# Expert rows scattered to their token's place and read back plainly, empty slots skipped, alpha in the first norm's parameters

## The chip, the cores and the metric

The kernel runs on one core of one Trainium2 chip. The metric is device microseconds of one execution, the median of the runs. The engines are TensorE (PE, with its weight loads PEld), VectorE (DVE), ScalarE (ACT), GpSimd (POOL) and SyncE (SP, which here only issues transfers). A transfer issued by SyncE or ScalarE goes through a queue of its own (q1, q10), one issued by GpSimd through q0; 16 transfer engines serve all queues.

## The reference

The reference is one inference step of a decoder trunk of two layers for 512 prompt tokens and 64 sample tokens, together T = 576 tokens of D = 1024 numbers, all in float32. Cut to what matters here:

```python
def hier_moe(x, w_group, b_group, w_expert, b_expert, w_gate_up, w_down):
    ...
    top_vals, top_idx = lax.top_k(e_in_group, TOP_K_INNER)
    top_w = jax.nn.softmax(top_vals, axis=-1) * g_w[:, None]
    expert_id = g_idx[:, None] * EXPERTS_PER_GROUP + top_idx
    combine = jnp.sum(jax.nn.one_hot(expert_id, N_EXPERTS, dtype=jnp.float32) * top_w[..., None], axis=1)
    hgu = jnp.einsum("td,edf->tef", xt, w_gate_up)
    gate, up = jnp.split(hgu, 2, axis=-1)
    a = jax.nn.silu(gate) * up * combine.astype(x.dtype)[:, :, None]
    y = jnp.einsum("tef,efd->td", a, w_down)
    ...
        x = layer_norm(DEEPNORM_ALPHA * x + mix, ln1_g[i], ln1_b[i])
        moe = hier_moe(x, moe_w_group[i], moe_b_group[i], moe_w_expert[i], moe_b_expert[i],
                       moe_w_gate_up[i], moe_w_down[i])
        x = layer_norm(DEEPNORM_ALPHA * x + moe, ln2_g[i], ln2_b[i])
        gate = jax.nn.sigmoid(jnp.einsum("bsd,de->bse", x, ple_w_gate[i]) + ple_b_gate[i])
        x = x + gate * jnp.einsum("bsp,pd->bsd", p[i], ple_w_proj[i])
```

There are 16 experts, each token uses two, so a layer has 2 x 576 = 1152 pairs of token and expert. An expert has a gate_up matrix of 1024 x 512 and a down matrix of 256 x 1024.

## The kernel before

Every product is made of three products of high and low halves. ScalarE writes the high half of a weight unit (`w_hi`, line 678), VectorE the low half (`w_lo`, line 944). A unit is 128 x 2048 numbers, 1 MiB, in one of four buffers `w_raw`; SyncE loads unit d once unit d - 4 is split. An expert has three units, two for gate_up and one for down.

A layer runs its mixer, then the first norm (token tiles of 128, the fifth of 64), the router, the experts, the second norm and the gated projection (PLE). The code is written out for each engine, and semaphores order the engines; no scheduler moves anything.

First norm and router: TensorE turns the rows, ScalarE normalises them into `x_tok`, and GpSimd multiplies and adds the norm's parameters `ln_params` (lines 604 and 609, tile 3 on VectorE), then stores the rows in memory, `x_scratch` (line 598). The parameters are loaded at line 594. VectorE computes the ranks of tokens in their experts; a matrix product turns them into `slot_token`: for each expert 128 slots that hold the number of a token. An empty slot holds 0, so it gathers token 0's row. Line 1196 copies this table from PSUM.

Experts: GpSimd gathers the 128 rows of a slot tile from `x_scratch` into one of two buffers `x_gathered` (line 619, all 16 gathers in a row, each from the third on waiting until TensorE turned the tile before the last). TensorE's step s (`moe_step`, line 1736) is gate_up of expert s, turning the slots of s + 1 (line 1689), down of expert s - 1, turning the activations of s. ScalarE and VectorE write the halves `xgT_hi` and `xgT_lo` (lines 797 and 1245), the activation with SiLU (line 819), and ScalarE copies the result out of PSUM to `expert_y` (line 804) and issues its store to `y_scratch` (line 806), at row 128 s. `expert_y` has one buffer: the next copy waits for the store. Before the first expert ScalarE multiplies all of `x_tok` by alpha, lines 830 and 831. Where an expert has over 128 tokens, an overflow part runs under an `If`; with the reference's inputs it doesn't run.

Second norm: GpSimd waits for all stores and gathers for each of five token tiles twice the 128 rows that belong to its tokens (line 646, places in `token_slot`) into `y_gathered`, which has room for four tiles. VectorE adds both to `x_tok` with their weights (line 1309) and takes statistics; for tiles 3 and 4 ScalarE weights the first rows (line 872) and GpSimd adds them (line 653). ScalarE normalises, TensorE turns the rows. SyncE has issued the loads of `ple_w_gate` before and goes on to `b_w_in` of the next mixer in layer 0.

## Time and profile before

| | |
|---|---|
| median of 3 runs | 1434.43 us (1432.51 to 1435.21) |
| the profiled execution | 1434.39 us, span 1432.9 us |
| TensorE busy | 1278.4 us, 89% of the span |
| VectorE busy | 808.0 us, 56% |
| ScalarE busy | 582.6 us, 41% |
| GpSimd busy | 207.5 us, 14% |
| mean transfer rate | 170 GB/s, 244.25 MB |

The page gives shares of the whole span. The stages differ: the experts of the first layer run from about 598 to 776 us, those of the second from about 1144 to 1320 us. In the slices of part 2 these stand out by their GB/s. A timeline row gives the start of an operation or a run of equal ones, the time it took, the line, what it writes and reads, and in brackets how long its engine had been idle and what ended that.

### The profile page before, as it was taken

How to read it: one execution, taken by the hardware profiler on the slowest of the kernel's cores; microseconds unless marked ns; L12 is line 12 of the kernel's file. 1: busy time of each engine (PE TensorE's matmuls, PEld its weight loads, DVE VectorE, ACT ScalarE, POOL GpSimd, SP SyncE). 2: the span in 40 equal slices, each digit the busy share in tenths (PEclk: the TensorE clock that was granted, in tenths of full speed). 3: DMA queues.
4: the chain of work that ended last, by engine and by line, in shares of the span. 5: the costliest groups of instructions: out<-in, count | busy, mean ns of one | idle time of the engine just before them, and what ended most of it. 6: DMA issues, size and time to landing. Idle time of an engine off the chain costs nothing.

```text
span 1432.9 us, 21217 instructions
## 1 busy us (share of the span) xinstructions
PE 1278.4 (89%) x8445; PEld 1192.5 (83%) x8445; DVE 808.0 (56%) x1086; ACT 582.6 (41%) x616; POOL 207.5 (14%) x208
## 2 busy tenths in 40 slices
PE   5999999999999999799994297999999889996297
PEld 5999999999999998677883297999998778885297
DVE  4634356453553535778884744355334878885741
ACT  4322222213122123578884522212213488886422
POOL 2300110000000004211212200000004311211300
PEclk9999999999999999799997598999999889998599
DMA  9443334243242231489997421122112479997301
GB/s 313 140 152 122 108 106 137 70 147 106 70 135 77 73 113 45 183 331 412 419 422 272 138 80 43 60 89 89 45 56 96 166 267 423 420 423 282 123 1 66
DMA packets 92547, 244.25 MB, mean 170 GB/s; under 512 B 6070, under 2 KB 53342, under 8 KB 80064
## 3 DMA queue, kind: packets, MB, share of 16 engines
q1 hardware_dynamic: 71520, 170.40, 32.3%
q0 software_dynamic: 16352, 56.12, 11.5%
q10 hardware_dynamic: 4608, 16.78, 2.9%
q8 instruction: 48, 0.79, 0.2%
q14 instruction: 19, 0.16, 0.0%
HBM read 209.90 MB, written 33.37 MB: 170 GB/s over the span
## 4 chain that ended last, share of the span: by engine, by line
PE 76%; DVE 6%; ACT 6%; DMA 5%; issue 4%; POOL 2%; ACTq 0%; SPq 0%; DVEq 0%; POOLq 0%
PE ps L1408 18%; PE ps L1409 18%; PE ps L1410 17%; PE ps L1704 3%; PE ps L1705 3%; PE ps L1706 3%; ACT w_hi L678 2%; PE ps L1503 2%; POOL y_gathered L646 1%; DMA y_scratch<-expert_y 1%; DMA y_gathered<-y_scratch,token_slot 1%; PE ps L1721 1%; PE ps L1723 1%; PE ps L1722 1%; DVE w_lo L944 1%
## 5 line engine op out<-in xcount | busy, mean ns | idle before, releaser
L944 DVE TENSOR_TENSOR w_lo<-w_raw,w_hi 128x2048 fp32r<-128x2048 f32 (+1 forms) x164 | 359.6, 2210 | 123.7 <-ACT w_hi L678 122.5
L678 ACT ACTIVATE w_hi<-w_raw 128x2048 fp32r<-128x2048 f32 (+1 forms) x164 | 300.2, 1847 | 104.7 <-PE ps L1410 75.2
L1408 PE MATMUL ps<-x_hi,w_hi 128*128 128x288 f32 x1024 | 306.5, 299 | 11.5 <-DVE x_lo L1326 11.0
L1410 PE MATMUL ps<-x_hi,w_lo 128*128 128x288 f32 x1024 | 304.7, 298 | 0.0
L1409 PE MATMUL ps<-x_lo,w_hi 128*128 128x288 f32 x1024 | 304.5, 297 | 0.0
L1408 PEld LDWEIGHTS ps<-x_hi,w_hi 128*128 128x128 f32 x1024 | 195.2, 191 | 13.5 <-issue 11.3
L1409 PEld LDWEIGHTS ps<-x_lo,w_hi 128*128 128x128 f32 x1024 | 195.2, 191 | 0.0
L1410 PEld LDWEIGHTS ps<-x_hi,w_lo 128*128 128x128 f32 x1024 | 195.0, 190 | 0.0
L1408 PE MATMUL ps<-w_hi,x_hi 128*128 128x256 f32 x480 | 137.5, 286 | 4.0 <-DVE v_stage L984 4.0
L1409 PE MATMUL ps<-w_lo,x_hi 128*128 128x256 f32 x480 | 136.9, 285 | 0.0
L1410 PE MATMUL ps<-w_hi,x_lo 128*128 128x256 f32 x480 | 136.9, 285 | 0.0
L1704 PE MATMUL ps<-w_hi,xgT_hi 128*128 128x512 f32 x256 | 105.2, 411 | 17.7 <-DVE xgT_lo L1245 17.4
L1408 PE MATMUL ps<-g_hi,w_hi 128*128 128x288 f32 x384 | 115.2, 300 | 3.4 <-DVE g_full L1377 2.7
L1409 PE MATMUL ps<-g_lo,w_hi 128*128 128x288 f32 x384 | 114.0, 297 | 0.0
L1410 PE MATMUL ps<-g_hi,w_lo 128*128 128x288 f32 x384 | 113.5, 295 | 0.0
L1705 PE MATMUL ps<-w_lo,xgT_hi 128*128 128x512 f32 x256 | 101.6, 397 | 0.0
L1706 PE MATMUL ps<-w_hi,xgT_lo 128*128 128x512 f32 x256 | 101.5, 397 | 0.0
L619 POOL DMA_INDIRECT x_gathered<-x_scratch,slot_token x32 | 61.3, 1917 | 247.3 <-PE ps L1689 230.1
L1408 PEld LDWEIGHTS ps<-w_hi,x_hi 128*128 128x128 f32 x480 | 93.3, 194 | 4.1 <-issue 4.1
L1409 PEld LDWEIGHTS ps<-w_lo,x_hi 128*128 128x128 f32 x480 | 93.4, 194 | 0.0
L1410 PEld LDWEIGHTS ps<-w_hi,x_lo 128*128 128x128 f32 x480 | 93.2, 194 | 0.0
L1026 DVE TENSOR_TENSOR g_full<-g_full,ps 128x512 f32<-128x512 f32 x24 | 16.4, 685 | 123.0 <-PE ps L1505 123.0
(263 smaller groups left out, 2141.0 us busy)
## 6 DMA issues: line engine op xcount, KB each, us to landing
w_raw<-in_moe_w_gate_up SPq DMA_DIRECT2D x64, 1024.0 KB, 7.9
w_raw<-in_moe_w_down SPq DMA_DIRECT2D x32, 1024.0 KB, 9.4
w_raw<-in_a_w_in SPq DMA_DIRECT2D x24, 1024.0 KB, 5.3
y_scratch<-expert_y ACTq DMA_DIRECT2D x32, 512.0 KB, 8.1
w_raw<-in_a_w_out SPq DMA_DIRECT2D x12, 1024.0 KB, 5.1
w_raw<-in_b_w_in SPq DMA_DIRECT2D x12, 1024.0 KB, 5.2
w_raw<-in_ple_w_gate SPq DMA_DIRECT2D x8, 1024.0 KB, 8.2
v_scratch<-v_stage POOLq DMA_DIRECT2D x12, 512.0 KB, 3.5
```

The source lines that it names most:

```text
L619: pool.indirect_dma_start(out=xg[:, s % 2, :], out_offset=None, in_=x_dram[l][:, :], in_offset=bass.IndirectOffsetOnAxis(ap=idx[:, s:s + 1 ...
L646: pool.indirect_dma_start(out=yrows(i, tok(i), k), out_offset=None, in_=y_dram[l][0:rows, :], in_offset=bass.IndirectOffsetOnAxis(ap=pos_u ...
L678: act.activation(whi[:, j, 0:n], raw[:, j, 0:n], ACT.Copy).then_inc(hi_done, 1)
L944: dve.tensor_tensor(wlo[:, j, 0:n], raw[:, j, 0:n], whi[:, j, 0:n].bitcast(f32), ALU.subtract).then_inc(split_done, 1)
L1026: dve.tensor_tensor(gf[:, fl % 2, 0:TP], gf[:, fl % 2, 0:TP], ps[:, b, :], ALU.mult)
L1408: pe.matmul(out, sh, mh, start=first, stop=False)
L1409: pe.matmul(out, sh, ml, start=False, stop=False)
L1410: ins = pe.matmul(out, sl, mh, start=False, stop=final)
L1503: pe.matmul(ps[:, b, P * c:P * c + P], vc[:, c, P * fl:P * fl + P], wst[:, ds(h, 1), :].rearrange("p a t -> p (a t)"), start=False, stop=( ...
L1704: pe.matmul(ps[:, 0, :], xs[0], ws[0], start=(a == 0 and k == 0), stop=False)
L1705: pe.matmul(ps[:, 0, :], xs[0], ws[1], start=False, stop=False)
L1706: ins = pe.matmul(ps[:, 0, :], xs[1], ws[0], start=False, stop=(a == 1 and k == 3))
```

## The change

Four things are changed, in both layers.

The number that a slot carries is no longer a token but 2T minus the row k T + t, where k tells whether the expert is the token's first or second. An empty slot holds 0. From it VectorE computes two tables: `slot_token` (for an empty slot T, outside the rows) and `slot_row` (for an empty slot 2T). Gathers take bounds and skip rows outside them, so an empty slot moves nothing.

The results of an expert go to `y_scratch`, now 2T rows, at row k T + t, by a scatter that GpSimd issues, in place of ScalarE's plain store. The scatter of expert s - 4 stands behind the gather of expert s in GpSimd's queue. The second norm's rows then lie in order: SyncE reads a token tile's both rows with one plain transfer, five for a layer, between its loads of `ple_w_gate` and the next ones.

The norm's parameters are multiplied by alpha on GpSimd once, so that `x_tok`, `x_scratch` and what is gathered hold alpha x. ScalarE's two scalings go. SiLU takes 1 / alpha as its scale, and the weights of the rows are divided by alpha.

The computation of `token_slot` on VectorE moves into the overflow part.

```diff
-    y_dram = [nc.dram_tensor(f"y_scratch{l}", (SLOT_TILES * CAP, D), f32).ap() for l in range(DEPTH)]
+    y_dram = [nc.dram_tensor(f"y_scratch{l}", (2 * T, D), f32).ap() for l in range(DEPTH)]
...
                 for j in range(4):
                     load_unit(0, j, cols8(x_in["ple_w_gate"][l], 256 * j), shape=256, wait=U_G[l] + j - 3)
+
+                sp.wait_ge(eu_used, EU * (l + 1))
+                sp.wait_ge(etl_ok, 2 * NE * (l + 1))
+                sp.wait_ge(y_st, 16 * NE * (l + 1))
+                y_rows = y_dram[l].rearrange("(k t) d -> t k d", k=2)
+                for i in range(NT):
+                    if i >= 4:
+                        sp.wait_ge(st_ok, 2 * NT * l + NT + i - 3)
+                    sp.dma_start(yg[0:tok(i), i % 4, :, :], y_rows[P * i:P * i + tok(i)]).then_inc(yg_ld[i % 4], 16)
...
-            ch.link(pool.iota(tokid[:, :], pattern=[[P, NT]], base=0, channel_multiplier=1, allow_small_or_imprecise_dtypes=True))
-            pool.memset(tokid[TS:P, 4:5], 0.0)
+            ch.link(pool.iota(rowval[:, :, :], pattern=[[-T, 2], [-P, NT]], base=2 * T, channel_multiplier=-1, allow_small_or_imprecise_dtypes=True))
...
                 pool.wait_ge(ln_ld, 32 * (l + 1))
+                pool.tensor_scalar(lnp[:, :, :], lnp[:, :, :], ALPHA, None, ALU.mult).then_inc(ln_ok, 1)
+                pool.wait_ge(ln_ok, l + 1)
...
-                                            in_offset=bass.IndirectOffsetOnAxis(ap=idx[:, s:s + 1], axis=0)).then_inc(xg_ld[s % 2], 16)
-
-                for s in range(NE):
+                                            in_offset=bass.IndirectOffsetOnAxis(ap=idx[:, s:s + 1], axis=0),
+                                            bounds_check=T - 1, oob_is_err=False).then_inc(xg_ld[s % 2], 16)
+
+                def scatter(s, sem_):
+                    pool.indirect_dma_start(out=y_dram[l][:, :], out_offset=bass.IndirectOffsetOnAxis(ap=row_idx[:, s:s + 1], axis=0),
+                                            in_=y_sb[:, :], in_offset=None, bounds_check=2 * T - 1, oob_is_err=False).then_inc(sem_, 16)
+
+                def expert_rows(s):
+                    pool.wait_ge(y_cp, NE * l + s + 1)
+                    scatter(s, y_st)
+
+                for s in range(4):
                     gather(s)
...
+                pool.wait_ge(row_ok, l + 1)
+                for s in range(4, NE):
+                    gather(s)
+                    expert_rows(s - 4)
+                for s in range(NE - 4, NE):
+                    expert_rows(s)
...
-                    act.wait_ge(y_cp, q + 1)
-                    act.dma_start(y_dram[l][ds(it * (P * step) + P * s, P), :], y_sb[:, :]).then_inc(y_st, 16)
...
-                        act.activation(act_a[:, 0, :], ps[:, 0, 0:F], ACT.Silu).then_inc(si_ok, 1)
+                        act.activation(act_a[:, 0, :], ps[:, 0, 0:F], ACT.Silu, scale=1 / ALPHA).then_inc(si_ok, 1)
...
-                act.wait_ge(x_st, 16 * NT * (l + 1))
-                act.activation(xtok[:, 0:4, :], xtok[:, 0:4, :], ACT.Copy, scale=ALPHA)
-                act.activation(xtok[0:TS, 4, :], xtok[0:TS, 4, :], ACT.Copy, scale=ALPHA).then_inc(xs_ok, 1)
...
-                dve.tensor_copy(idx[:, 0:NE], ps[:, 6, 256:256 + NE]).then_inc(idx_ok, 1)
+                row_v = ps[:, 6, 256:256 + NE]
+                ch.link(dve.tensor_scalar(shift[:, 0:NE], row_v, T + 0.5, float(T), ALU.is_ge, ALU.mult))
+                dve.scalar_tensor_tensor(out=idx[:, 0:NE], in0=shift[:, 0:NE], scalar=float(T), in1=row_v, op0=ALU.add, op1=ALU.subtract).then_inc(idx_ok, 1)
+                dve.tensor_scalar(row_idx[:, 0:NE], row_v, -1.0, 2.0 * T, ALU.mult, ALU.add).then_inc(row_ok, 1)
...
+                ch.link(dve.tensor_scalar(gm[:, 3, :], gm[:, 3, :], ALPHA, None, ALU.mult))
                 ch.link(dve.reciprocal(wtop[:, 0, :], gm[:, 3, :]))
```

How it stands on the engines, at three places. GpSimd, from the first norm's last rows to the expert loop, before (`x_gathered` is filled by line 619, `n_overflow` is the count of overflow tiles):

```order
L609 TENSOR_TENSOR x_tok<-x_tok,ln_params 64x1024
L598 DMA x_scratch<-x_tok 64x1024
L619 DMA x_gathered<-x_scratch,slot_token 128x1024 x16
L625 TENSOR_LOAD n_overflow
L625 ISA x2
L626 COMPARE_AND_BRANCH
```

The same place now; lines 630 and 635 are the gather and the scatter:

```order
L620 TENSOR_TENSOR x_tok<-x_tok,ln_params 64x1024
L607 DMA x_scratch<-x_tok 64x1024
L630 DMA x_gathered<-x_scratch,slot_token 128x1024 x5
L635 DMA y_scratch<-expert_y,slot_row 1152x1024
L630 DMA x_gathered<-x_scratch,slot_token 128x1024
L635 DMA y_scratch<-expert_y,slot_row 1152x1024
```

The sixteen gathers that stood in one row now alternate with sixteen scatters, from the fifth on.

ScalarE, from the router's exponential to expert 0, before:

```order
L791 ACTIVATE softmax<-softmax 128x5
L830 ACTIVATE x_tok<-x_tok 128x4096
L831 ACTIVATE x_tok<-x_tok 64x1024
L797 ACTIVATE xgT_hi<-ps 128x512 x2
L678 ACTIVATE w_hi<-w_raw 128x2048 x2
```

And now:

```order
L801 ACTIVATE softmax<-softmax 128x5
L807 ACTIVATE xgT_hi<-ps 128x512 x2
L688 ACTIVATE w_hi<-w_raw 128x2048 x2
L827 ACT_TABLE_LOAD
L827 ACTIVATE expert_act<-ps 128x256
```

The two scalings of `x_tok` are gone from between the exponential and the first copy.

SyncE, after the experts' loads of the first layer, before (`w_raw` are the four unit buffers):

```order
L397 DMA w_raw<-in_ple_w_gate 128x8x256 x4
L473 UNCONDITIONAL_BRANCH
L473 ISA
L397 ISA
L397 DMA w_raw<-in_b_w_in 128x8x256
```

And now:

```order
L398 DMA w_raw<-in_ple_w_gate 128x8x256 x4
L481 DMA y_gathered<-y_scratch 128x2x1024 x4
L481 DMA y_gathered<-y_scratch 64x2x1024
L483 UNCONDITIONAL_BRANCH
L483 ISA
L398 ISA
L398 DMA w_raw<-in_b_w_in 128x8x256
```

The five reads of expert rows stand ahead of the loads of `b_w_in`.

## Rows read from the trace of the kernel before

**Rows 1.** page part 2: GB/s moved in 40 equal slices.

```profile
GB/s 313 140 152 122 108 106 137 70 147 106 70 135 77 73 113 45 183 331 412 419 422 272 138 80 43 60 89 89 45 56 96 166 267 423 420 423 282 123 1 66
```

**Rows 2.** windows: us, busy us, PEclk, DMA share, GB/s.

```profile
700.00:720.00 20.00, 19.53 (x94) 16.17 (x94) 17.20 (x14) 17.11 (x17) 4.26 (x2) 1.00 1.02 422
```

**Rows 3.** chain of waits: start us, us, what; two of the steps.

```profile
1187.13 0.96 PE ps L1689 x8
...
1296.69 0.96 PE ps L1689 x8
```

**Rows 4.** timeline, TensorE, one step: start us, us, line, operation [idle before].

```profile
646.12 0.49 PE L1704 MATMUL ps<-w_hi,xgT_hi 128*128 128x512 f32 x1 [0.77 <-DVE xgT_lo L1245]
...
655.62 0.49 PE L1704 MATMUL ps<-w_hi,xgT_hi 128*128 128x512 f32 x1
```

**Rows 5.** timeline, ScalarE, first layer, start of the expert stage.

```profile
599.27 3.60 ACT L830 ACTIVATE x_tok<-x_tok 128x4096 f32<-128x4096 f32 x1
...
603.72 1.05 ACT L797 ACTIVATE xgT_hi<-ps 128x512 fp32r<-128x512 f32 x2
```

**Rows 6.** timeline, TensorE, same place, then the second layer.

```profile
599.02 1.22 PE L1689 MATMUL ps<-ident,x_gathered 128*128 128x128 f32 x8 [1.97 <-DMA x_gathered<-x_scratch,slot_token]
605.74 0.80 PE L1704 MATMUL ps<-w_hi,xgT_hi 128*128 128x512 f32 x1 [5.50 <-DVE xgT_lo L1245]
...
1146.05 1.92 PE L1689 MATMUL ps<-ident,x_gathered 128*128 128x128 f32 x8 [3.20 <-DMA x_gathered<-x_scratch,slot_token]
1151.54 0.79 PE L1704 MATMUL ps<-w_hi,xgT_hi 128*128 128x512 f32 x1 [3.57 <-DVE xgT_lo L1245]
```

**Rows 7.** timeline, VectorE, first layer, same place.

```profile
604.40 1.29 DVE L1245 TENSOR_TENSOR xgT_lo<-ps,xgT_hi 128x512 fp32r<-128x512 f32 x2 [4.20 <-ACT xgT_hi L797]
```

**Rows 8.** line 619, the row gather: durations in ns, issue to landing.

```profile
L619 POOL DMA_INDIRECT x_gathered<-x_scratch,slot_token x32: 932/2044/3064, 589.0 to 1278.2; - x32
...
DMA to landing us min/median/max: 4.1/10.3/12.2
```

**Rows 9.** the store's line 806: issue to landing.

```profile
DMA to landing us min/median/max: 2.7/8.1/9.3
```

**Rows 10.** transfers: what, queue, count, KB each, us to landing.

```profile
w_raw<-in_b_w_in SPq DMA_DIRECT2D x12, 1024.0 KB, 5.2
...
out<-y_rows SPq DMA_DIRECT2D x4, 512.0 KB, 2.6
...
out<-y_rows SPq DMA_DIRECT2D x1, 256.0 KB, 2.9
```

**Rows 11.** chain of waits: last stores of both layers, one copy before.

```profile
772.88 2.65 DMA y_scratch<-expert_y
...
1309.24 1.03 ACT expert_y L804
...
1316.98 2.67 DMA y_scratch<-expert_y
```

**Rows 12.** timeline, GpSimd: first norm, then the first read of expert rows.

```profile
540.71 2.40 POOL L604 TENSOR_TENSOR x_tok<-x_tok,ln_params 128x1024 f32<-128x1024 f32 x1 [13.49 <-PE ps L1586]
...
776.52 2.78 POOL L646 DMA_INDIRECT y_gathered<-y_scratch,token_slot  x1 [40.92 <-DMA y_scratch<-expert_y]
```

**Rows 13.** timeline, VectorE: the second norm of both layers.

```profile
776.20 6.70 DVE L944 TENSOR_TENSOR w_lo<-w_raw,w_hi 128x2048 fp32r<-128x2048 f32 x3 [9.08 <-ACT w_hi L678]
788.45 2.60 DVE L1309 SCALAR_TENSOR_TENSOR x_tok<-y_gathered,top_weights,x_tok 128x1024 f32<-128x1024 f32 x2 [5.55 <-DMA y_gathered<-y_scratch,token_slot]
...
802.01 2.08 DVE L1084 SCALAR_TENSOR_TENSOR neg_mean_rstd<-mean_var,rstd 128x1 f32<-128x1 f32 x1
804.18 1.28 DVE L1309 SCALAR_TENSOR_TENSOR x_tok<-y_gathered,top_weights,x_tok 128x1024 f32<-128x1024 f32 x1
...
1329.37 2.60 DVE L1309 SCALAR_TENSOR_TENSOR x_tok<-y_gathered,top_weights,x_tok 128x1024 f32<-128x1024 f32 x2 [2.56 <-DMA y_gathered<-y_scratch,token_slot]
...
1344.94 1.28 DVE L1309 SCALAR_TENSOR_TENSOR x_tok<-y_gathered,top_weights,x_tok 128x1024 f32<-128x1024 f32 x1
```

More of the change, by code:

```diff
@@ L212, in trunk @@
     amat = xt("slot_onehot", [P, 2, NT, P], f32r)
-    tok16 = xt("choice_tokens", [P, 2, NT, NE], f32r)
+    tok16 = xt("choice_rows", [P, 2, NT, NE], f32r)
+    shift = xt("choice_shift", [P, SLOT_TILES])
     m16 = xt("expert_onehot", [P, NZ, NE], f32r)
@@ L298, in trunk @@
         y_cp, y_st = sem("y_copied"), sem("y_stored")
-        ov = [{n: sem(f"ovf_{n}{l}") for n in ("parts", "onehot", "idx", "idxcopied", "turned", "copied", "gu", "silu", "a", "aturned", "acopied", "y", "ycopied", "stored")} for l in range(DEPTH)]
+        ov = [{n: sem(f"ovf_{n}{l}") for n in ("chain", "parts", "onehot", "idx", "idxcopied", "turned", "copied", "gu", "silu", "a", "aturned", "acopied", "y", "ycopied", "stored")} for l in range(DEPTH)]
         sg_ok, pe_ok = sem("gate_ready"), sem("layer_done")
@@ L848, in _ @@
                         act.wait_ge(o["gu"], i + 1)
-                        act.activation(act_a[:, 0, :], ps[:, 0, 0:F], ACT.Silu).then_inc(o["silu"], 1)
+                        act.activation(act_a[:, 0, :], ps[:, 0, 0:F], ACT.Silu, scale=1 / ALPHA).then_inc(o["silu"], 1)
                         act.wait_ge(o["aturned"], i + 1)
@@ L1279, in _ @@
                     o = ov[l]
+                    och = Chain(dve, o["chain"])
+                    och.link(dve.tensor_tensor(nov[:, 2, :], incl, nov[:, 0, :], ALU.subtract))
+                    och.link(dve.scalar_tensor_tensor(out=nov[:, 2, :], in0=nov[:, 2, :], scalar=float(CAP), in1=ovf_base[:, :], op0=ALU.mult, op1=ALU.add))
+                    for a, b in GROUPS:
+                        ins = dve.scalar_tensor_tensor(out=post[:, a:b, :], in0=ranks_of(a, b), scalar=float(CAP),
+                                                       in1=nov[:, 2, :].unsqueeze(1).to_broadcast([P, b - a, NE]), op0=ALU.is_ge, op1=ALU.mult)
+                    och.link(ins)
+                    och.link(dve.tensor_tensor(post[:, :, :], post[:, :, :], iota_e[:, :].unsqueeze(1).to_broadcast([P, NT, NE]), ALU.add))
+                    for k in range(2):
+                        ins = dve.tensor_tensor(t16[:, k, :, :], oh16[:, k, :, :], post[:, :, :], ALU.mult)
+                    och.link(ins)
+                    och.link(dve.tensor_reduce(out=pmd[:, 0, :, :].rearrange("p k t -> p (k t)"), in_=t16[:, :, :, :].rearrange("p k t e -> p (k t) e"),
+                                              op=ALU.add, axis=AX.X))
+                    och.link(dve.tensor_tensor(pmd[:, 0, :, :], pmd[:, 0, :, :], rk[:, :, :], ALU.add))
                     dve.tensor_copy(posi[:, 0, :, :], pmd[:, 0, :, :]).then_inc(o["parts"], 1)
@@ L1293, in _ @@
                     dve.wait_ge(o["idx"], 1)
-                    dve.tensor_copy(idx[:, NE:], ps[:, 6, 0:OVF]).then_inc(o["idxcopied"], 1)
+                    ovf_v = ps[:, 6, 0:OVF]
+                    och.link(dve.tensor_scalar(shift[:, NE:], ovf_v, T + 0.5, float(T), ALU.is_ge, ALU.mult))
+                    dve.scalar_tensor_tensor(out=idx[:, NE:], in0=shift[:, NE:], scalar=float(T), in1=ovf_v, op0=ALU.add, op1=ALU.subtract)
+                    dve.tensor_scalar(row_idx[:, NE:], ovf_v, -1.0, 2.0 * T, ALU.mult, ALU.add).then_inc(o["idxcopied"], 1)
                     with dve.Fori(0, OVF) as i:
```

85 lines of the change are left out of this document (28 added, 57 removed).

## The prediction

> **What bounds the kernel now.** I read first where the transfers are dense. The slices of 35.8 us show 412 to 423 GB/s in two stretches, one for each layer's experts, and less elsewhere [rows 1]. A 20 us window inside such a stretch has the transfer engines at share 1.02, TensorE busy 19.53 us at clock 1.00, VectorE 17.20, ScalarE 17.11 [rows 2]. So in the expert loop two things are nearly full at once. The loop's step is the distance between turnings of slots in the chain: 11 steps from 1187.13 to 1296.69, (1296.69 - 1187.13) / 11 = 9.96 us [rows 3]. One step of TensorE with hardly a wait in it takes 655.62 - 646.12 = 9.50 us, its floor at full clock [rows 4]. Bytes a step: 3 MiB of weights, 0.5 MiB gathered, 0.5 MiB stored, 4.19 MB, which at 422 GB/s is 9.9 us. The rest of the two stages is a head (slots turned, expert 0 begins) and a tail (last expert's rows stored, read back, second norm), where TensorE stands still and single operations follow one another; there a microsecond removed is a microsecond of the kernel.
>
> **The change part by part.** Sums are made against the profiled execution, 1434.39 us (span 1432.9), which is the median of the three runs (1434.43) within 0.04.
>
> Head. ScalarE's two scalings of x_tok go: from 599.27 to the first xgT_hi at 603.72 it is 4.45 us [rows 5]. What is late next is the turning of slot 0: 599.02 to 600.24 in the first layer, 1146.05 to 1147.97 in the second [rows 6]. The first copy starts about when the turning's first half is done, so that the second half is ready 0.53 us later (half of 1.05): at 599.8 and 1147.4. From that copy to gate_up of expert 0 it takes 605.74 - 603.72 = 2.02 us, VectorE's subtraction at 604.40 included [rows 5 to 7]. That gives 601.8 and 1149.5 in place of 605.74 and 1151.54. VectorE now needs one operation more before the slot indices are ready, about 0.2 us with its link, and the gathers start so much later. Gain: 605.74 - 602.0 = 3.7 and 1151.54 - 1149.7 = 1.8, together **5.5 us**. Bounds: 0 if the gather lands later by as much, 8.9 if it were there at once. The small overflow operations that leave VectorE stand beside TensorE's projections and count for nothing, as does the longer softmax by one operation.
>
> First norm. GpSimd multiplies the 128x2048 parameters by alpha. The trace has no such operation; the 128x1024 one took 2.40 us [rows 12], so 0 to 4.8 us. GpSimd stood idle for 13.49 us before its first product [rows 12], and the parameters land inside that: hidden. What it can cost is a small VectorE operation held behind it, as one was held for 2.08 us at 802.01 [rows 13]; TensorE turns and multiplies meanwhile. I take 0, bound 2.1 a layer. SiLU's scale and the factor in the weights ride along at 0.
>
> Steady loop. The gathers move 1152 rows a layer instead of 2048, the stores too. If the time followed the bytes, a step would need 3.15 + 2 x 0.295 = 3.74 MB, 8.9 us, and TensorE's 9.50 would bound it: -0.46 us a step. But 512 KB on 128 partitions took 2.6 us and 256 KB on 64 partitions 2.9 [rows 10]: fewer partitions were no faster. Slots fill from partition 0 up, so the low partitions carry as much as before, and I give the relief no value. Against it stands the way of the rows out. Now ScalarE itself issues the store, which lands in 8.1 us [rows 9]: with the copy's 1.03 [rows 11] 9.1 of the 9.96, it just fits. Behind the change GpSimd issues it: an indirect transfer takes GpSimd 0.93 to 3.06 us and lands, that included, in 10.3 [rows 8]. expert_y has one buffer, so 1.03 + 0.3 + 10.3 = 11.6 us between copies is the upper bound, +1.7 us a step. For it speak the gathers; against it, that gather and scatter follow each other in one queue, so that two queues share the engines where three did, and that ScalarE no longer waits and issues between its copy and the next product. With about 13 steps a layer that feel it, 26 in all, the ends are -12 and +44 us. I take **0**: a turnaround near 10 us, about the present step.
>
> The Trainium skill, page "SBUF — State Buffer", section "Summary: rules for kernel authors", speaks against this part: a transfer whose descriptors GpSimd writes should not be hidden under VectorE's work but issued from ScalarE or SyncE. The trace agrees that GpSimd's issue varies (0.93 to 3.06 us, rows 8); by the rule each of the 32 scatters pays the long issue, which is the first rival below.
>
> Tail. The last two scatters replace stores with little traffic beside them. The quickest indirect transfer landed in 4.1 us, the quickest store in 2.7 [rows 8, 9]; with 0.3 us for GpSimd to start each costs 4.1 + 0.3 - 2.7 = 1.7 more. Both count, the last but one because the last copy waits for its buffer: the last rows lie in memory at 772.88 + 2.65 + 3.4 = 778.9 and 1316.98 + 2.67 + 3.4 = 1323.1 [rows 11]. Then SyncE reads plain megabytes; one lands in 5.2 us [rows 10], with 0.2 to wake: 784.3 and 1328.5. In place of that GpSimd began at 776.52, with 2.78 us for the first of ten gathers [rows 12], and VectorE started at 788.45 and 1329.37 [rows 13]. Its w_lo work ended at 782.9 and moves by at most 1.7, so it is no bound. Gain 4.1 and 0.9. Further on, token tile 3 started 804.18 - 788.45 = 15.7 and 15.6 us after tile 0 [rows 13], since its rows came last and ScalarE's weighting waited for them. With the rows there at 2.5 us a megabyte (1 MiB at 422 GB/s), it follows the chain of engines: two tiles on VectorE of about 4.2 us (two products of 1.3 and the statistics), ScalarE's normalisation and weighting of 1.2 each, GpSimd's addition of 2.4 [rows 12] and small steps, 13.5: 2.2 and 2.1 less. Together **9.3 us**. SyncE's queue: the next layer's weights of b_w_in stand behind the five reads, which wait for the last scatter and for the first statistics. They are first converted while the gate's tiles run, long after the norm: hidden, and out of the way of the reads.
>
> Sum: 5.5 + 0 + 0 + 9.3 = 14.8; 1434.4 - 14.8 = **1419.6 us**.
>
> **The rivals.** (1) The turnaround of expert_y becomes the bound, the slower case. At 11.6 us a step all 26 steps lose 1.7: 1463.8. With part of the wait off, say +0.9, 1443. It decides from 14.8 / 26 = 0.57 us a step, a turnaround of 10.5 us. For it: 9.1 us already fits with only 0.8 left. Against: fewer bytes and one queue fewer.
>
> (2) The relief works. Then the step falls to 9.50: 1419.6 - 26 x 0.46 = 1407.6. For it: 7.4 MB a layer not moved. Against: rows 10. By the Trainium skill, page "DMA: Bandwidth & Descriptors", section "The descriptor swizzle", partitions 0 to 63 of a transfer belong to eight of the sixteen engines. The router on the reference's inputs gives 42 to 110 slots an expert, so these eight would still move 7.6 of 8 rows on average and the step would fall by 0.1 us only, 1417. No row here shows single engines.
>
> (3) The change doesn't bring what it says in head and tail: the indirect transfers with skipped rows take GpSimd longer, and the first gather and the last scatter come late by what is saved. With 3 us lost at each of the four places, 1431.6.
>
> **How the numbers follow.** Forecast, step unchanged within 0.2 us (1414 to 1425): 0.45. Relief: 0.20. Turnaround: 0.22. Nothing in head and tail: 0.13. The range reaches from 1405, under the relief case by the bounds of the head, to 1440, into the turnaround case; half of that case and the best of the relief stay out. A measurement of this kernel tells 0.2%, 2.9 us, from no change. Faster by more: 0.45 + 0.20 + 0.08 of the last case = 0.73; within: 0.05 of the last case and 0.01 of the turnaround case = 0.06; slower: the other 0.21.
>
> **What would show it.** In the changed kernel's profile gate_up of expert 0 should start 3.0 and 3.6 us after the turning of slot 0 instead of 6.7 and 5.5 [rows 6], the steps in the chain should stand 9.8 to 10.1 us apart, ScalarE's copy of expert_y should wait for the scatter by less than 0.3 us, VectorE's first product of the second norm should come 10 to 12 us after the last copy of expert_y begins, and tile 3 13.5 us after tile 0. Steps of 10.5 us or more with waits of expert_y for the scatter are rival 1; steps of 9.5 and a transfer share well under 1 are rival 2. I would be wrong if a scatter to memory costs much more than a gather, for no row here shows one.

## The result and the profile after

The changed kernel takes 1419.85 us, median of six runs (1416.29 to 1426.59), beside 1435.37 for the kernel before in the same session (1432.51 to 1436.74). The ratio is 0.9896, 95% interval 0.987 to 0.9922: 1.0% faster. The prediction was 1419.6 us.

One profiled execution of each kernel stands behind what follows; of the changed kernel it took 1416.81 us (span 1415.3), the lower end of its runs, so 17.6 us of span are explained and not 15.5. The six runs spread over 10 us, so that a median within 0.3 us of the forecast is in part luck. Lines have moved: the gather is L630, the scatter L635, the copy to expert_y L814, the turning of slots L1699, gate_up L1714 to L1716, the first product of the second norm L1319.

The page of the changed kernel: GB/s in 40 slices, the two large DMA queues, the shares of the chain that ended last by engine and by line.

```profile
GB/s 288 148 175 96 137 96 148 72 126 85 116 137 70 82 62 83 169 270 352 365 377 280 198 90 35 60 91 90 45 57 96 160 262 365 370 372 261 134 1 67
q1 hardware_dynamic: 73984, 179.84, 36.1%
q0 software_dynamic: 18336, 48.79, 10.0%
PE 66%; DMA 20%; DVE 6%; ACT 5%; issue 2%; POOL 0%; POOLq 0%; SPq 0%; DVEq 0%; ACTq 0%
PE ps L1418 18%; PE ps L1420 18%; PE ps L1419 18%; DMA y_scratch<-expert_y,slot_row 17%; ACT expert_y L814 2%; PE ps L1513 2%; DVE x_tok L1319 1%; PE ps L1576 1%; PE ps L1578 1%; PE ps L1577 1%; DVE w_lo L947 1%; DMA w_raw<-in_a_w_in 1%; DVE v_stats L1322 1%; PE ps L1714 1%; PE ps L1515 1%
```

The expert slices move 352 to 377 GB/s where [rows 1] had 412 to 423, as the skipped rows should have it. But the chain has a new owner. The scatters hold 17% of it: through most of both expert loops the chain goes copy, scatter, copy, scatter. A window inside the loop (us, busy us with counts, clock, share, GB/s), to be held against [rows 2]:

```profile
700.00:720.00 20.00, 18.95 (x90) 15.53 (x90) 16.91 (x15) 15.79 (x16) 6.01 (x4) 1.00 0.97 363
```

TensorE does a little less in the same time (18.95 us for 19.53), at the same clock of 1.00. The share of the transfer engines hardly fell (0.97 for 1.02) while the bytes moved in the window fell by 14%: this share doesn't say how much more could be moved.

Where the 17.6 us came from, by stretches between the same events in both traces. "Slots" is the start of the VectorE instruction that writes slot_token, "first copy" and "last copy" are ScalarE's copies to expert_y of experts 0 and 15, "first product" is VectorE's first of the second norm, "xT" is the start of ScalarE's last copy to xT:

| stretch, us | before, layer 0 / 1 | after, layer 0 / 1 | change, both | predicted |
|---|---|---|---|---|
| slots to first copy (head) | 37.71 / 37.82 | 33.81 / 34.00 | -7.7 | -5.5 |
| first to last copy (15 steps) | 146.19 / 144.37 | 147.02 / 148.89 | +5.3 | +3.4 |
| last copy to first product | 16.62 / 13.44 | 10.30 / 10.08 | -9.7 | -8.4 |
| first product to xT | 28.80 / 28.65 | 26.35 / 26.35 | -4.8 | -4.3 |
| all the rest | | | -0.8 | 0 |

The prediction's tail of 9.3 us is spread here over three lines: it charged 1.7 us a layer for the last scatter but one, which falls into the 15 steps, and 1.7 for the last one, which falls into the line below. The second line hides two changes of opposite sign: the first 13 steps of both layers together are 6.9 us longer, the last two 1.6 us shorter.

### The profile page after: what moved, and what is told of

It reads as the page before. It is cut to its first block, busy times and chain, and to the rows that moved or that the text cites. A ratio compares the mean times of both kernels' runs of the same rounds, so it can differ in the third digit from the quotient of the medians.

```text
span 1415.3 us, 21194 instructions
## 1 busy us (share of the span) xinstructions
PE 1275.4 (90%) x8445; PEld 1188.7 (84%) x8445; DVE 802.1 (57%) x1072; ACT 567.6 (40%) x612; POOL 220.6 (16%) x221
## 4 chain that ended last, share of the span: by engine, by line
PE 66%; DMA 20%; DVE 6%; ACT 5%; issue 2%; POOL 0%; POOLq 0%; SPq 0%; DVEq 0%; ACTq 0%
PE ps L1418 18%; PE ps L1420 18%; PE ps L1419 18%; DMA y_scratch<-expert_y,slot_row 17%; ACT expert_y L814 2%; PE ps L1513 2%; DVE x_tok L1319 1%; PE ps L1576 1%; PE ps L1578 1%; PE ps L1577 1%; DVE w_lo L947 1%; DMA w_raw<-in_a_w_in 1%; DVE v_stats L1322 1%; PE ps L1714 1%; PE ps L1515 1%
## 5 line engine op out<-in xcount | busy, mean ns | idle before, releaser
L1418 PEld LDWEIGHTS ps<-x_hi,w_hi 128*128 128x128 f32 x1024 | 194.6, 190 | 13.5 <-issue 11.3
L1714 PE MATMUL ps<-w_hi,xgT_hi 128*128 128x512 f32 x256 | 105.2, 411 | 16.6 <-DVE xgT_lo L1238 16.5
L1716 PE MATMUL ps<-w_hi,xgT_lo 128*128 128x512 f32 x256 | 101.8, 398 | 0.0
L630 POOL DMA_INDIRECT x_gathered<-x_scratch,slot_token x32 | 59.2, 1850 | 146.1 <-PE ps L1699 129.1
```

The costliest lines, as they stand in the source:

```text
L630: pool.indirect_dma_start(out=xg[:, s % 2, :], out_offset=None, in_=x_dram[l][:, :], in_offset=bass.IndirectOffsetOnAxis(ap=idx[:, s:s + 1 ...
L1418: pe.matmul(out, sh, mh, start=first, stop=False)
L1714: pe.matmul(ps[:, 0, :], xs[0], ws[0], start=(a == 0 and k == 0), stop=False)
L1716: ins = pe.matmul(ps[:, 0, :], xs[1], ws[0], start=False, stop=(a == 1 and k == 3))
```

## What the trace of the changed kernel shows

**Head.** The timeline of TensorE, ScalarE and GpSimd at the start of the expert stages (start us, us, line, operation, idle before):

```profile
599.42 1.20 PE L1699 MATMUL ps<-ident,x_gathered 128*128 128x128 f32 x8 [1.91 <-DMA x_gathered<-x_scratch,slot_token]
...
602.23 0.80 PE L1714 MATMUL ps<-w_hi,xgT_hi 128*128 128x512 f32 x1 [1.61 <-DVE xgT_lo L1238]
...
1131.96 1.20 PE L1699 MATMUL ps<-ident,x_gathered 128*128 128x128 f32 x8 [2.12 <-DMA x_gathered<-x_scratch,slot_token]
1134.76 0.79 PE L1714 MATMUL ps<-w_hi,xgT_hi 128*128 128x512 f32 x1 [1.60 <-DVE xgT_lo L1238]
...
600.18 1.08 ACT L807 ACTIVATE xgT_hi<-ps 128x512 fp32r<-128x512 f32 x2 [0.35 <-PE ps L1699]
...
533.05 5.40 POOL L610 TENSOR_SCALAR ln_params<-ln_params 128x2048 f32<-128x2048 f32 x1 [4.66 <-DMA ln_params<-in_ln_b]
541.79 2.38 POOL L615 TENSOR_TENSOR x_tok<-x_tok,ln_params 128x1024 f32<-128x1024 f32 x1 [3.34 <-PE ps L1596]
```

gate_up now follows the turning by 2.8 us in both layers, where it took 6.7 and 5.5 [rows 6]; ScalarE waits for the turning, not the turning for ScalarE. The new multiply on GpSimd takes 5.40 us, over the bound of 4.8, and is hidden: after it GpSimd still waits 3.34 us before its first product.

The turning itself has changed in layer 1: 1.92 us before and 1.20 now. The granted clock of TensorE in that stretch was 0.54 before, after 3.20 us without work, and 0.96 now, after 2.12 us (in layer 0 0.93 and 0.98). So the faster turning of layer 1 is 0.7 us of the head.

**Loop.** The copy's line (durations in ns, then what its engine waited for before it: us, times), then the scatter's line and its landing, then two steps of the chain:

```profile
L814 ACT ACTIVATE expert_y<-ps x32: 1023/1027/1034, 622.4 to 1303.8; 128x1024 f32<-128x1024 f32 x32
...
  DMA y_scratch<-expert_y,slot_row: 58.5, 29
  PE ps L1733: 5.9, 3
```

```profile
L635 POOL DMA_INDIRECT y_scratch<-expert_y,slot_row x32: 973/1002/1240, 624.3 to 1305.6; - x32
...
DMA to landing us min/median/max: 3.2/8.2/9.5
```

```profile
643.21 1.04 ACT expert_y L814
...
644.30 0.74 issue
645.04 8.89 DMA y_scratch<-expert_y,slot_row
...
653.95 1.04 ACT expert_y L814
...
655.04 0.74 issue
655.78 8.20 DMA y_scratch<-expert_y,slot_row
```

Nearly every copy waits some 2 us for the scatter of the one before: 1.04 for the copy, 0.8 until GpSimd's transfer starts, 8.2 to land (median, with the 1.0 us in which GpSimd issues it), 10.0 in all. The copies of experts 0 and 13 start 132.5 us apart, 10.19 a step (before: 130.3, 10.02), in the second layer 10.28 (before: 9.92).

**Tail.** The chain behind the last copy of layer 0, then VectorE's timeline: its first products of tiles 0 and 3 there, and of tile 0 in layer 1.

```profile
769.43 1.03 ACT expert_y L814
...
771.23 3.26 DMA y_scratch<-expert_y,slot_row
...
774.57 5.05 DMA y_gathered<-y_scratch
...
779.73 1.29 DVE x_tok L1319
```

```profile
779.73 2.60 DVE L1319 SCALAR_TENSOR_TENSOR x_tok<-y_gathered,top_weights,x_tok 128x1024 f32<-128x1024 f32 x2 [0.64 <-DMA y_gathered<-y_scratch]
...
793.02 1.29 DVE L1319 SCALAR_TENSOR_TENSOR x_tok<-y_gathered,top_weights,x_tok 128x1024 f32<-128x1024 f32 x1
...
1313.89 2.60 DVE L1319 SCALAR_TENSOR_TENSOR x_tok<-y_gathered,top_weights,x_tok 128x1024 f32<-128x1024 f32 x2 [0.54 <-DMA y_gathered<-y_scratch]
```

VectorE starts 10.3 and 10.1 us after the last copy (before 16.6 and 13.4), and tile 3 follows tile 0 by 13.3 us instead of 15.7. No run changes the tail alone. But in the table below the nine other kernels with plain reads, whatever else they do, need 9.6 to 11.0 us from the last copy to the first product, and the one that keeps GpSimd's ten gathers (alpha alone) 16.0 and 13.8.

## The experiments

All times are medians of five or six runs. The ratio is to the kernel before in the same session, with its 95% interval. The stretches are those of the table above, from one profiled execution, whose span stands beside.

| kernel | us | ratio | span | head | 15 steps | to first product |
|---|---|---|---|---|---|---|
| changed | 1419.85 | 0.9896 (0.987 to 0.9922) | 1415.3 | 33.8 / 34.0 | 147.0 / 148.9 | 10.3 / 10.1 |
| alpha alone, on before | 1428.19 | 0.9954 (0.9941 to 0.9967) | 1425.1 | 34.8 / 34.9 | 145.4 / 145.7 | 16.0 / 13.8 |
| plain store | 1412.8 | 0.9854 (0.9834 to 0.9873) | 1411.2 | 33.8 / 34.1 | 146.2 / 144.9 | 11.0 / 10.8 |
| no skip | 1426.18 | 0.9938 (0.9924 to 0.9952) | 1425.3 | 36.4 / 37.0 | 149.5 / 149.5 | 10.3 / 10.2 |
| skip in the scatter alone | 1420.57 | 0.9898 (0.9873 to 0.9924) | 1425.1 | 34.3 / 35.0 | 151.3 / 149.2 | 10.2 / 10.1 |
| alternate halves | 1418.2 | 0.9876 (0.9861 to 0.9892) | 1415.7 | 33.8 / 34.6 | 148.4 / 146.0 | 10.1 / 9.6 |
| two buffers | 1409.44 | 0.9818 (0.9805 to 0.9831) | 1408.1 | 34.0 / 33.9 | 143.5 / 143.5 | 10.1 / 10.3 |
| two buffers, no skip | 1415.08 | 0.9853 (0.9829 to 0.9878) | 1413.5 | 36.8 / 37.3 | 142.7 / 143.2 | 10.2 / 10.2 |
| two buffers, alternate halves | 1401.24 | 0.9765 (0.9747 to 0.9784) | 1399.1 | 33.9 / 34.6 | 137.3 / 138.7 | 10.4 / 10.2 |
| two buffers, runs of 16 | 1406.92 | 0.9796 (0.9775 to 0.9816) | 1406.5 | 34.0 / 34.7 | 142.1 / 141.6 | 10.1 / 10.5 |
| two buffers, even partitions | 1400.72 | 0.9755 (0.9734 to 0.9777) | 1403.9 | 33.7 / 34.8 | 139.5 / 145.2 | 10.4 / 9.7 |

Three profiled executions lie at the slow end of their kernel's runs: skip in the scatter alone (1426.7 us, its median is 1420.6), even partitions (1405.4 for 1400.7) and runs of 16 (1408.1 for 1406.9). Their stretches are read with that in mind. The longer spans of a few kernels sit in the loops; the tail hardly varies.

### Two buffers for expert_y

```diff
     y_sb = xh("expert_y", [P, D], f32, 20480)
+    y_two = [y_sb, xh("expert_y1", [P, D], f32, 24576)]
...
-                        act.wait_ge(y_st, q * 16)
-                    act.activation(y_sb[:, :].rearrange("p (b t) -> p b t", b=2), ps[:, 4:6, :], ACT.Copy).then_inc(y_cp, 1)
+                        act.wait_ge(y_st[s % 2], it * (8 * step) + 16 * ((NE * l + s) // 2))
+                    act.activation(y_two[s % 2][:, :].rearrange("p (b t) -> p b t", b=2), ps[:, 4:6, :], ACT.Copy).then_inc(y_cp, 1)
```

The second buffer lies where only the overflow path has a tile.

> The changed kernel with a second expert_y buffer: ScalarE's copy of expert s goes to buffer s mod 2 and waits for the scatter of expert s-2, not of s-1. In the changed kernel that copy waited 58.5 us for scatters, in 29 waits of about 2 us. Theory (the turnaround of the one buffer, 1.04 us of copy + 0.8 us until the scatter starts + 8.2 us of landing = 10.0 us, is what ends the step): the waits go to under 5 us in all, the distance from one copy to the next falls from 10.19 us towards the 9.5 to 9.7 us of TensorE's work, and 26 steps give back 9 to 17 us: 1403 to 1411 us. Rival (the transfers are the bound, the wait for the scatter only stands where a wait for weights would stand): the 58.5 us turn up as waits of ScalarE and VectorE for w_raw, the step stays 10.1 to 10.3 us, 1417 to 1421 us.

Measured: 1409.44 us, 10.4 less than the changed kernel; the intervals of the ratios are apart. The copy's line and what it waits for:

```profile
L817 ACT ACTIVATE expert_y<-ps x32: 1002/1024/1034, 624.0 to 1296.4; 128x1024 f32<-128x1024 f32 x32
...
  PE ps L1737: 15.7, 14
```

The 58.5 us of waits for the scatter are gone, and the 15 steps fall by 3.5 and 5.4 us (the two profiled executions are 7.2 us apart, the medians 10.4, since the changed kernel's was one of its fastest). So the turnaround of the one buffer did bound the changed kernel's loop. The time lies in the theory's range, its step doesn't: 10.0 us between copies of experts 0 and 13, not 9.5 to 9.7. What came next is in this kernel's chain of waits:

```profile
684.84 1.93 ACT w_hi L691
...
697.80 1.93 ACT w_hi L691
699.75 2.30 DVE w_lo L951
702.21 9.74 DMA w_raw<-in_moe_w_down
711.98 1.93 ACT w_hi L691
713.93 2.30 DVE w_lo L951
716.40 8.67 DMA w_raw<-in_moe_w_gate_up
...
738.84 1.92 ACT w_hi L691
```

This is the ring of the four w_raw buffers: a weight transfer of 8 to 10 us, 1.9 for w_hi, 2.3 for w_lo, and only then the next transfer into that buffer. The four turns from 684.84 to 738.84 take 13.5 us each. A turn serves four transfers and a step needs three, which gives 10.1 us a step beside the 10.0 measured. (The 13.1 us in an expectation further down are the shorter of these turns.)

### The plain store in place of the scatter

```diff
-    pool.wait_ge(y_cp, NE * l + s + 1)
-    scatter(s, y_st)
...
+    act.wait_ge(y_cp, q + 1)
+    act.dma_start(y_dram[l][ds(it * (P * step) + P * s, P), :], y_sb[:, :]).then_inc(y_st, 16)
```

This kernel leaves out the placing: its rows stay in the order of the slots, and what is added at the end are other rows.

> The changed kernel with the plain store of the kernel before in place of the scatter: ScalarE issues it right behind its copy, 128 rows to 16 fixed places; the plain reads at the end stay (they read the first 1152 rows of that store, so the rows that are added up at the end are other rows: the placing is left out), the skip in the gather and the part on alpha stay. One expert_y buffer. Theory (what the loop lost is the way over GpSimd, 0.8 us of start and an issue of 1.0 us, in the turnaround of the one buffer): ScalarE's wait for the buffer falls from 58.5 us to under 10, the 15 distances of copy to copy fall from 147.0 and 148.9 us back to 144 to 146.5, and the whole to 1412 to 1416 us. Rival (the waits come from the transfers' length, whoever issues them): waits over 40 us, 1418 to 1422 us.

Measured: 1412.8 us, 7 less than the changed kernel and inside the theory's range; the intervals of the two ratios just touch. What the copy waited for:

```profile
  PE ps L1734: 12.8, 10
  DMA y_scratch<-expert_y: 7.2, 4
```

The store lands no faster in the loop (8.1 us median, the scatter 8.2), but it starts some 0.15 us after the copy and moves all 128 rows of each expert, 2048 for the 1152 of the scatter. The waits fall from 58.5 to 7.2 us, the 15 steps go back to 146.2 and 144.9. What the scatter costs with one buffer is mainly its start through another engine, inside a turnaround that had under 1 us to spare. That the store also has a queue of its own was not separated from it.

### No skip, and a skip in the scatter alone

```diff
-                dve.scalar_tensor_tensor(out=idx[:, 0:NE], in0=shift[:, 0:NE], scalar=float(T), in1=row_v, op0=ALU.add, op1=ALU.subtract).then_inc(idx_ok, 1)
+                ch.link(dve.scalar_tensor_tensor(out=tok_f[:, :], in0=shift[:, 0:NE], scalar=float(T), in1=row_v, op0=ALU.add, op1=ALU.subtract))
+                dve.tensor_scalar(idx[:, 0:NE], tok_f[:, :], float(T - 1), None, ALU.min).then_inc(idx_ok, 1)
```

This stands in both. For no skip at all, empty slots also get rows of their own behind the 1152 in y_scratch.

> The changed kernel without the skipping: an empty slot gathers the last token's row, and its row of expert_y is scattered to a row of its own behind the 1152 that are read back. All 128 rows move in each of the 32 gathers and the 32 scatters, as many bytes as in the kernel before. Two small VectorE instructions more (about 0.3 us) stand before the slots are known. Theory (the skip was worth little, since the transfer engines of the lower partitions carry the same rows with or without it): 1419 to 1424 us, moved bytes back to 410 to 425 GB/s in the loop with the same share of 1.0. Rival (the skip carries the loop, and the scatter without it costs what the bytes say, 14% of a step's transfers): landing of the scatter over 10 us, steps over 10.8 us, 1430 us and more, and then the gain would be lost without it.

> The changed kernel with the skip in the scatter alone: an empty slot gathers the last token's row, so all 128 rows move in every gather (one small VectorE instruction more, about 0.2 us). Theory (what the skip is worth stands in the first gathers of each layer, which nothing covers): the time from slot_token to the first copy of expert_y grows from 33.8 and 34.0 us to 36 or more, 4 to 6 us over the changed kernel, 1423.5 to 1426 us. Rival (it stands in the scatter's turnaround): that time stays within 1 us, 1420 to 1422 us.

Measured: 1426.18 and 1420.57 us. No skip costs 6.3 us, between the two ranges given. With the skip in the scatter alone no difference to the changed kernel can be told, as the rival had it. Without skip the DMA view of 640 to 740 us gives:

```profile
DMA packets 6977, 40.79 MB, mean 408 GB/s; under 512 B 782, under 2 KB 782, under 8 KB 3216
```

beside 365 GB/s in the changed kernel, for 13 steps of 10.27 and 10.25 us (10.19 and 10.28 with the skip). The bytes left out buy almost nothing in the loop. The two profiled executions are 10.0 us apart, of which 3.1 stand in the 30 steps and 5.6 in the heads, where they came as a surprise: the first gather lands after 11.15 us without skip (chain of waits) and after about 9.7 in the changed kernel (589.72 to the turning at 599.42). With all rows gathered but the scatter skipping, the head is 34.3 and 35.0 us only. So by this run 0.5 to 1 us a layer of head belong to the gather's skip. A part of the rest lies in the small VectorE instructions that the run without skip has more. Layer 0 of the changed kernel, then of the one without skip:

```profile
588.77 2.28 DVE L947 TENSOR_TENSOR w_lo<-w_raw,w_hi 128x2048 fp32r<-128x2048 f32 x1
589.72 2.32 POOL L630 DMA_INDIRECT x_gathered<-x_scratch,slot_token  x1 [8.21 <-DVE slot_token L1201]
```

```profile
588.45 2.28 DVE L949 TENSOR_TENSOR w_lo<-w_raw,w_hi 128x2048 fp32r<-128x2048 f32 x1
588.93 2.79 POOL L632 DMA_INDIRECT x_gathered<-x_scratch,slot_token  x1 [8.44 <-DVE slot_token L1204]
```

In both GpSimd ends its issue 0.99 us after VectorE's w_lo ends. Without skip w_lo starts 0.5 us later behind the slots, and so the issue ends 0.5 us later. From there the turning starts after 8.5 and 9.6 us (7.4 and 7.6 with the skip), and gate_up another 0.6 us later, since the turning takes 1.95 us at a granted clock of 0.50 instead of 1.20. With the scatter alone skipping the turning starts 8.0 and 9.1 us after the issue; why it comes later still without any skip stays open.

### Two buffers without the skip

> Two expert_y buffers without the skipping: all 128 rows move in every gather and scatter. Against the changed kernel the same edit cost 6.3 us (1426.2 to 1419.9), of which 5.6 us stood ahead of the first copy of expert_y in the two layers and 3.1 us in the loops. Theory (the skip shortens the first gathers, and with one buffer little else; in the loop the moved rows lengthen the weight transfers little): 1414 to 1418 us, the 15 distances of copy to copy under 145.5 us. Rival (once the turnaround is gone the loop is bound by transfers, and 14% more bytes show in every step): 1420 us and more, distances over 147 us.

Measured: 1415.08 us, 5.6 over the kernel with two buffers (the intervals just touch), in the theory's range. The 15 steps are 142.7 and 143.2, not longer than with the skip (143.5), though 419 GB/s are moved instead of 371; the difference is again in the head. Even with the turnaround out of the way, skipping rows in this layout gives the loop nothing.

### The alpha part alone

This puts the ALPHA edits of the diff on the kernel before: the multiply of ln_params, Silu's scale, the factor in the weights, and no multiply of x_tok on ScalarE.

> The kernel before with the part on alpha alone: alpha in the first norm's parameters (one multiply on GpSimd), the two ScalarE multiplies of 3.60 and 1.0 us gone, Silu with scale 1/alpha, weights divided by alpha. The store, the gathers of ten rows at the end and the unskipped slots stay. Theory (ScalarE's multiplies stood on the path into each expert loop, 3.7 us in layer 0 and 1.8 in layer 1, and nothing later takes it back): 5.5 us less than the kernel before, 1428.5 to 1431 us. Rival (the loop is bound by transfers that had started anyway, so an earlier start of it is made up by waits for weights): under 1.5 us less, 1434 to 1435.5 us.

Measured: 1428.19 us, 6.75 less than the kernel before, a little more than the range. The head falls by 2.9 and 3.0 us, the loops and the tail change by under 1 us each way, but for the second layer's loop (1.3 longer). An earlier start is not made up by later waits: the head's 5.9 us arrive in the whole.

### The same rows on other partitions

Rank r of an expert lies on partition r, and the experts have 42 to 110 rows. Four kernels lay the same ranks elsewhere, in three layouts; a permuted row of numbers in the comparison that makes slot_onehot does it. The edits are those of alternate halves (even ranks on partitions 0 to 63, odd ones on 64 to 127), of runs of 16 (the first 64 ranks on 0 to 15, 32 to 47, 64 to 79 and 96 to 111) and of even partitions:

```diff
-                        ins = dve.tensor_tensor(amat[:, k, a:b, :], iota[:, :].unsqueeze(1).to_broadcast([P, n, P]),
+                        for h in range(2):
+                            ins = dve.tensor_tensor(amat[:, k, a:b, 64 * h:64 * h + 64],
+                                                    iota[:, :].rearrange("p (b a) -> p a b", a=2)[:, h, :].unsqueeze(1).to_broadcast([P, n, 64]),
...
+            pool.iota(rank_at[:, :], pattern=[[32, 2], [16, 2], [64, 2], [1, 16]], base=0, channel_multiplier=0, allow_small_or_imprecise_dtypes=True)
...
+            pool.iota(rank_at[:, :], pattern=[[1, 64], [64, 2]], base=0, channel_multiplier=0, allow_small_or_imprecise_dtypes=True)
```

First with one buffer:

> The changed kernel with each expert's rows laid on other partitions: rank r goes to partition r/2 for even r and 64 + r/2 for odd r, where it went to partition r. The same 1152 rows and the same bytes move; the counts of the experts (42 to 110, mean 72) fill on average 36 of the lower 64 partitions and 36 of the upper 64, where they filled 60 and 12. Theory (the rows left out relieve nothing because those that are left lie on the partitions, and so on the transfer engines, that were full already): the landing of the scatter falls from 8.2 us to 5 to 7 us and the gather's from 9.5 to 6 to 8, the step falls by 0.2 to 0.6 us, 1404 to 1414 us. Rival (it does not matter on which partitions the rows lie): landings within 0.5 us of 8.2 and 9.5, step 10.2 us, 1418 to 1422 us.

Measured: 1418.2 us, 1.6 less than the changed kernel with intervals that overlap; between 640 and 740 us the scatter lands in 8.2 us as before, the gather in 9.1. By its numbers the rival. Yet the copy still waited 43.5 us for scatters, so what the weight transfers gained (7.7 us to landing for 8.1 in the same window) could not shorten the step. That question came back with the second buffer:

> Two expert_y buffers (1409.4 us) together with the rows laid alternately on the lower and upper 64 partitions (alone: 1.6 us less than the changed kernel). In the run with two buffers the chain goes through the four w_raw buffers: a weight transfer of 8.5 to 9.5 us, 1.9 us of w_hi, 2.3 us of w_lo, then the next transfer into that buffer, 13.1 us for four transfers at three a step, 9.85 us a step. Theory (with the buffer's turnaround gone the weight transfers are the bound, and rows on all partitions shorten the longest of them): step from 10.0 to 9.7 us, 1402 to 1407 us. Rival (the partitions do not matter, the 1.6 us were a difference of one run to another): 1408 to 1411 us.

Measured: 1401.24 us, 8.2 below two buffers alone, intervals apart, a little better than the theory's range. A window of the kernel with two buffers, then the same window here:

```profile
680.00:700.00 20.00, 19.22 (x93) 15.79 (x92) 17.06 (x15) 16.58 (x16) 6.69 (x4) 1.00 0.97 378
```

```profile
680.00:700.00 20.00, 20.00 (x98) 16.86 (x97) 18.39 (x15) 17.52 (x19) 4.27 (x4) 1.00 1.00 388
```

TensorE is busy 20.00 of 20 us. The copies of layer 0 stand 9.54 us apart, those of layer 1 9.65: this is the 9.50 us floor of [rows 4], nearly reached. What changed is the weights, as the DMA view of 640 to 740 us shows, first with two buffers in order, then alternate:

```profile
w_raw<-in_moe_w_gate_up SPq DMA_DIRECT2D x20, 1024.0 KB, 8.8
```

```profile
w_raw<-in_moe_w_gate_up SPq DMA_DIRECT2D x20, 1024.0 KB, 7.4
```

They land 1.4 us sooner. Which pattern of partitions does it was left to two more kernels.

> Two expert_y buffers, and the first 64 ranks of an expert laid on partitions 0 to 15, 32 to 47, 64 to 79 and 96 to 111, the other 64 on the partitions between (made once, by one more GpSimd iota at the start). So the occupied rows lie half in the lower 64 partitions and half in the upper 64, as in the run with alternate halves (1401.2 us), but in runs of 16 partitions. Theory A (what counts is that both halves of 64 carry rows): 1400 to 1403 us, distances of copy to copy 9.5 us. Theory B (what counts is a finer pattern, one that repeats every 32 partitions and of which this layout fills half): as with two buffers and ranks in order, 1407 to 1411 us, distances of 10.0 us. The Trainium skill, 'DMA: Bandwidth & Descriptors', section 'The descriptor swizzle', states such a pattern: four neighbouring partitions and the four that lie 32 above them belong to one engine, and by it this layout reaches 8 of the 16 engines with its first 64 ranks, as the layout in order does; theory B is what that rule would give.

> Two expert_y buffers, and the first 64 ranks of an expert laid on the 64 even partitions, the other 64 on the odd ones. Theory A and B of the run before this one both give 1400 to 1403 us here (both halves of 64 are filled alike, and so is every group of four partitions, to a half). Rival (it is the alternation of the lower and upper half from one rank to the next that counts, since neighbours in rank then go to places far apart): 1407 to 1411 us.

Measured: 1406.92 us with runs of 16, steps of 9.9 us: near theory B, with a part of the gain at most. 1400.72 us with even partitions: as good as alternate halves, though neighbours in rank stay close together. By the times it is neither the halves of 64 nor the distance of neighbours, but a finer pattern in the partition number: all five runs with even partitions (1399.5 to 1405.4) are below all five with runs of 16 (1405.9 to 1408.1), though the intervals of the ratios just touch. ScalarE's w_hi waits for weight transfers, 640 to 740 us in layer 0 (us in total, times, longest), go the same way; two buffers in order, runs of 16, even partitions, alternate halves:

```profile
ACT w_hi L691 <- DMA w_raw<-in_moe_w_gate_up: 12.5, 14, 1.6
```

```profile
ACT w_hi L693 <- DMA w_raw<-in_moe_w_gate_up: 10.7, 12, 1.3
```

```profile
ACT w_hi L693 <- DMA w_raw<-in_moe_w_gate_up: 5.6, 8, 1.1
```

```profile
ACT w_hi L691 <- DMA w_raw<-in_moe_w_gate_up: 1.8, 3, 1.0
```

Layer 1 doesn't bear this out. In the profiled execution with even partitions, the slowest of its five, that wait is 13.3 us between 1180 and 1280 us, against 10.9 with runs of 16 and 5.5 with alternate halves, and its steps are 10.1 us. So the finer pattern rests on the times and on layer 0.

The Trainium skill, page "DMA: Bandwidth & Descriptors", section "The descriptor swizzle", gives such a pattern: eight partitions, four neighbours and the four that lie 32 above, go to one transfer engine. By that rule the first 64 ranks fill 8 engines with eight rows each where they lie in order or in runs of 16, and put four rows on each of the 16 in the other two layouts; the times agree (1409.4 and 1406.9 against 1401.2 and 1400.7). No row here shows single engines, so the rule is borne out by times, not seen.

## Why the prediction was right, and where it was not

**The total** is off by 0.3 us, which is in part luck: errors of both signs stand under it. Of the 17.6 us of span it had 14.8: the gains of head and tail were undersized by 4.0 us, the loss of the loop by 1.9, and 0.8 came from elsewhere. The loop's error is itself a balance. The steady loop was put at nothing and cost 6.9 us in its first 13 steps of each layer; the last scatter but one was charged 3.4 us, and the last two steps came out 1.6 us shorter than before. With those 6.9 us put right and nothing else the forecast would have been 1426.5.

**Head: right in kind, too small.** 5.5 us predicted, 7.7 found, of which the alpha part alone gives 5.9. Layer 1 is the miss (1.8 predicted, 3.8 found). gate_up was to follow the turning by 3.0 and 3.6 us and does by 2.8 in both, since the turning of layer 1 takes 1.20 us at a granted clock of 0.96 and no longer 1.92 at 0.54 [rows 6]. The step that failed is the one that left the gather where it was but for 0.2 us: in layer 1 the turning starts 11.0 us after the slots are known (1120.92), before 12.3 (1133.74 to 1146.05), in layer 0 10.8 and 11.1. Of the 2.2 us more than forecast the gather gave 1.5 and the way from turning to gate_up 1.0, and 0.4 were lost between gate_up and the copy. The multiply on GpSimd was costed at nothing behind 13.49 us of idle time; that held, with a duration beyond the bound given.

**Loop: near in value, the mechanism missed.** The prediction put the turnaround near 10 us, and it is 10.0, but it had no sum for that value, which was chosen between the 9.1 of the store and the upper bound of 11.6. It concluded "about the present step" and that the copy would wait under 0.3 us: it waits about 2 us, 29 times. Of the terms of the upper bound, GpSimd started after 0.8 us and not 0.3, and the landing took 8.2 us and not 10.3. The gathers' 10.3 hold a long issue, which the scatters escape here because nearly all of them start when VectorE has no w_lo under way or has almost finished one (the last section shows it). A step of 10.0 us was bound elsewhere before, so the same length with another owner looks alike in the sum, and the chain then shows the scatter at 17%. The steps came out at 10.19 and 10.28, above the 9.8 to 10.1 announced. Rival 1 was at work in small, 0.17 and 0.36 a step, below its deciding 0.57.

**Relief by fewer bytes: rightly given no value.** Leaving the skip out costs 0.1 us a step with one buffer and none with two. The reason named, that slots fill from partition 0 up and low partitions stay full, is the one that the layouts bear out. What the prediction missed is the other side of it: spread over the partitions, the same bytes do bring the loop near TensorE's floor (9.54 and 9.65 a step), rival 2's 9.50. That needs the second buffer as well: with one buffer the spread rows gave 1.6 us, within the noise.

**Tail: right, one term mis-sized.** From the last copy to the first product a gain of 8.4 us was expected and 9.7 found. The last scatter landed in 3.26 us instead of 4.1, the read in 5.05 where 5.2 was taken, GpSimd started after 0.8 us and not 0.3. The last scatter but one was charged 1.7 us a layer and cost nothing: the two steps from the copy of expert 13 to that of expert 15 take 14.5 and 15.3 us, before 15.9 and 15.5. Tile 3 stands 13.3 us behind tile 0, forecast 13.5.

**Rival 3** (head and tail bring nothing) has fallen with the signatures above.

## What to carry to other kernels

When a transfer out of a single buffer moves to another engine, add up the buffer's whole turnaround (copy, start, landing) and compare it with the step: where it only just fits, 0.8 us of start become a chain of waits. A second buffer costs 4 KB a partition and gave 10.4 us here. When rows are left out of a transfer, ask on which partitions the remaining ones lie: bytes skipped at one end of the partitions gave the loop next to nothing, the same rows spread evenly gave 8.2 us more once there was a second buffer, and the best kernels of this study (1400.7 and 1401.2 us) need both edits. A sum that comes out right can hide a new owner of the chain; the next change has to start from the new chain, not from the old one.

## What the runs showed of the hardware

- A GpSimd tensor_scalar on 128x2048 f32 takes 5.40 us, for twice the elements 2.25 times the 2.40 us of its tensor_tensor on 128x1024 [rows 12].
- What GpSimd needs to issue an indirect transfer depends on VectorE. In layer 0 of the changed kernel the scatters take 0.97 to 1.24 us and the gathers 0.99 to 2.88, and each of those that starts while w_lo runs ends 0.84 to 0.99 us after w_lo ends. It is not a matter of gather or scatter: with two buffers the copies stand elsewhere in the step, the scatters start inside w_lo, and they take up to 1.92 us. VectorE's w_lo and the scatter beside it in that kernel:

```profile
663.31 2.28 DVE L951 TENSOR_TENSOR w_lo<-w_raw,w_hi 128x2048 fp32r<-128x2048 f32 x1
664.57 1.92 POOL L637 DMA_INDIRECT y_scratch<-expert_y,slot_row  x1 [1.81 <-ACT expert_y L817]
```

```profile
L637 POOL DMA_INDIRECT y_scratch<-expert_y,slot_row x32: 973/1316/1916, 625.8 to 1298.2; - x32
```

- The scatter's 128-row instruction lands like the plain store in the loop (8.2 and 8.1 us), and in 3.2 us when little else moves.
- The busy share of the transfer engines was 0.97 to 1.02 at 363, 388 and 422 GB/s alike. It says that transfers are under way, not that no more would fit.
